# Stick-breaking attention on one Trainium2 core: the causal mask added by VectorE in PSUM instead of by bf16 mask products on TensorE

## The reference, cut to what matters

```
z = einsum('bhtd,bhsd->bhts', qb, kb) * scale
strict = s_idx < t_idx
log_1m = where(strict, log_sigmoid(-z), 0.0)
suffix = cumsum(log_1m, axis=3, reverse=True) - log_1m
a = where(strict, exp(log_sigmoid(z) + suffix), 0.0)
out = einsum('bhts,bhsd->bhtd', a, vb)
```

## Time and profile before

| | before |
|---|---|
| median of 3 runs | 1301.5 us |
| the profiled execution's own time | 1301.93 us |
| its span | 1299.9 us |
| TensorE busy | 1281.9 us, 99% |
| VectorE busy | 883.7 us, 68% |
| ScalarE busy | 688.1 us, 53% |
| GpSimd busy | 110.7 us, 9% |

### The profile page before, as it was taken

One profiled execution on the slowest core, in us unless ns is written; L12 is line 12 of the kernel. 1 busy time (PEld: TensorE's weight loads), 2 busy tenths in 40 slices (PEclk: granted clock), 3 DMA queues, 4 the chain that ended last, 5 costly groups with the idle time before them and its releaser, 6 DMA issues.

```text
span 1299.9 us, 17608 instructions
## 1 busy us (share of the span) xinstructions
PE 1281.9 (99%) x7273; PEld 1106.5 (85%) x7273; DVE 883.7 (68%) x1038; ACT 688.1 (53%) x961; POOL 110.7 (9%) x176
## 2 busy tenths in 40 slices
PE   7999999999999999999999999999999999999999
PEld 7888897988888888888888888898877888888887
DVE  4656664776666776875676666768785566887775
ACT  5755544544444656564554444565566654654453
POOL 6200100100000100030100000101330003000000
PEclk9999999999999999999999999999999999999999
DMA  8754643565555553353365555563544435365552
GB/s 265 258 162 157 204 146 126 178 194 195 193 186 185 181 163 129 131 192 132 130 195 193 189 186 183 182 193 106 162 147 147 160 130 194 131 204 186 193 195 97
DMA packets 156112, 223.62 MB, mean 172 GB/s; under 512 B 6103, under 2 KB 107635, under 8 KB 156032
## 3 DMA queue, kind: packets, MB, share of 16 engines
q1 hardware_dynamic: 154240, 218.18, 51.0%
q0 software_dynamic: 1664, 4.27, 1.0%
q10 hardware_dynamic: 128, 0.05, 0.0%
HBM read 221.44 MB, written 1.05 MB: 171 GB/s over the span
## 4 chain that ended last, share of the span: by engine, by line
PE 85%; DVE 7%; ACT 4%; issue 2%; POOL 1%; DMA 1%; SPq 0%; POOLq 0%; ACTq 0%; DVEq 0%
PE ps L422 18%; PE ps L424 9%; PE ps L472 8%; PE ps L474 7%; PE ps L473 7%; PE ps L407 5%; PE ps L409 5%; PE ps L408 5%; PE ps L606 4%; PE ps L607 4%; PE ps L608 4%; DVE wlo L1691 3%; ACT whi L1149 2%; PE ps L493 1%; PE ps L541 1%
## 5 line engine op out<-in xcount | busy, mean ns | idle before, releaser
L1691 DVE TENSOR_TENSOR wlo<-raw,whi 128x1024 fp32r<-128x1024 f32 x409 | 491.6, 1231 | 167.9 <-ACT whi L1149 165.1
L1149 ACT ACTIVATE whi<-raw 128x1024 fp32r<-128x1024 f32 x412 | 425.5, 1052 | 334.7 <-PE ps L422 156.1
L422 PE MATMUL ps<-RR,whi 128*128 128x512 f32 x1024 | 353.8, 396 | 0.7 <-DVE ar L1794 0.7
L424 PE MATMUL ps<-RR,wlo 128*128 128x256 f32 x1024 | 264.8, 279 | 0.1
L472 PE MATMUL ps<-whi,RR 128*128 128x512 f32 x592 | 238.2, 402 | 2.1 <-DVE RR L1968 0.4
L474 PE MATMUL ps<-whi,RR 128*128 128x512 f32 x592 | 231.0, 390 | 0.0
L473 PE MATMUL ps<-wlo,RR 128*128 128x512 f32 x592 | 230.9, 390 | 0.0
L422 PEld LDWEIGHTS ps<-RR,whi 128*128 128x128 f32 x1024 | 184.8, 188 | 36.3 <-DVE ar L1794 1.0
L424 PEld LDWEIGHTS ps<-RR,wlo 128*128 128x128 f32 x1024 | 193.0, 188 | 11.9 <-DVE RR L1721 0.4
L407 PE MATMUL ps<-RR,whi 128*128 128x256 f32 x512 | 147.4, 288 | 1.5 <-DVE RR L1721 1.4
L409 PE MATMUL ps<-RR,wlo 128*128 128x256 f32 x512 | 144.8, 283 | 0.0
(11 more groups left out here) (338 smaller groups left out, 1266.7 us busy)
## 6 DMA issues: line engine op xcount, KB each, us to landing
raw<-in_ffn_w_gate_up SPq DMA_DIRECT2D x44, 1024.0 KB, 5.1
raw<-in_ffn_w_down SPq DMA_DIRECT2D x33, 1024.0 KB, 5.0
raw<-in_w_in SPq DMA_DIRECT2D x28, 1024.0 KB, 5.1
raw<-in_ffn_w_up SPq DMA_DIRECT2D x22, 1024.0 KB, 5.1
raw<-in_xa_w_kv SPq DMA_DIRECT2D x16, 1024.0 KB, 5.2
raw<-in_sb_w_qkv SPq DMA_DIRECT2D x12, 1024.0 KB, 5.1
raw<-in_ml_w_in SPq DMA_DIRECT2D x11, 1024.0 KB, 6.5
raw<-in_xa_w_q SPq DMA_DIRECT2D x8, 1024.0 KB, 5.3
```

The source lines that it names most:

```text
L422: m = pe.matmul(two(ps[:, bank, :]), p.hi[:, k, :], XT2[:, k, :, :], start=k == 0, stop=k == 7)
L424: pe.matmul(ps[:, bank, 0:256], p.lo[:, k, :], X.h[:, k, :], start=False, stop=False)
L1149: act.activation(p.hi, p.raw, ACT.Copy).then_inc(S["w_hi"], 1)
L1691: dve.tensor_tensor(p.lo, p.raw, p.hi.bitcast(F32), ALU.subtract).then_inc(S["w_lo"], 2 if p.n == 2 else 1)
```

## The change

- On TensorE the four mask products of each pair go. The first score product now starts the bank (`start=True`).
- On VectorE a new function `sb_mask(p)` adds `mStr` to both diagonal squares of both banks in one instruction, 128 partitions by 512 columns, read from PSUM and written back to PSUM, with the bf16 mask broadcast over the four squares. It waits until all scores of the pair are there (`sb_z`), and counts a new semaphore `sb_m`.
- On ScalarE `sb_logs(p)` waits for `sb_m` instead of `sb_z`.
- GpSimd builds `mStr` the other way round, since it is no longer transposed by a product. Same instructions.
- In VectorE's program, `sb_mask(p)` stands in front of `sb_sums(p)`, or of `sb_turned(p-1)` with `sb_sums(p)` right behind it. Around pair 4, one low part of a piece is made ahead of the mask and one behind it.

```diff
             def sb_scores(p):
...
                 for o, r in both:
-                    pe.matmul(o[:, 0:128], mStr[:, :], identb[:, :], start=True, stop=False, skip_group_check=True)
-                    pe.matmul(o[:, 256:384], mStr[:, :], identb[:, :], start=False, stop=False, skip_group_check=True)
-                for o, r in both:
-                    m = pe.matmul(o[:, 128:384], qT[r, p, 128:256], kT[r, p, :], start=False, stop=False, skip_group_check=True)
+                    m = pe.matmul(o[:, 128:384], qT[r, p, 128:256], kT[r, p, :], start=True, stop=False, skip_group_check=True)
                 m.then_inc(S["sb_z"], 1)
...
             def sb_logs(p):
-                act.wait_ge(S["sb_z"], 3 * p + 3)
+                act.wait_ge(S["sb_m"], p + 1)
...
+            def sb_mask(p):
+
+                b = 4 + 2 * (p % 2)
+                diagonal = ps[:, b:b + 2, :].rearrange("p b (x c) -> p b x c", c=128)[:, :, 0:3:2, :]
+                dve.wait_ge(S["sb_z"], 3 * p + 3)
+                dve.tensor_tensor(diagonal, diagonal, mStr[:, :].unsqueeze(1).unsqueeze(1).to_broadcast([128, 2, 2, 128]),
+                                  ALU.add).then_inc(S["sb_m"], 1)
...
             dve.wait_ge(*at("ones", 2))
+            dve.wait_ge(*at("masks", 3))
+            sb_mask(0)
             sb_sums(0)
             sb_k(1)
+            sb_mask(1)
             sb_sums(1)
...
             past("sbv0b")
+            sb_mask(2)
             sb_turned(1)
             sb_sums(2)
...
             lo_to(end("sbk2") - 1 + NSP)
+            sb_mask(3)
             sb_turned(2)
             sb_sums(3)
             sb_k(2)
+            lo_to(end("sbq3") - 1 + NSP)
+            sb_mask(4)
             past("sbq3")
             sb_turned(3)
...
             sb_rest(2)
+            sb_mask(7)
             sb_turned(6)
             sb_sums(7)
...
-            for m, cm, st_, base in ((mInc, -1, 1, 0), (mStr, -1, 1, -1), (mRow, 1, -1, 0)):
+            for m, cm, st_, base in ((mInc, -1, 1, 0), (mStr, 1, -1, -1), (mRow, 1, -1, 0)):
```

More of the change, by code:

```diff
@@ L29 @@
 ml_z mlv_act mlv_dve mo_add mt n_T n_hi n_lo n_r n_sq n_x out pa_m pa_r pa_sq pool_step resid row_in0 row_in1
-row_in2 row_in3 row_in4 row_in5 sb_a sb_c sb_hi sb_k sb_ln sb_lo sb_q sb_t sb_v sb_w sb_z sbv_act sbv_dve
+row_in2 row_in3 row_in4 row_in5 sb_a sb_c sb_hi sb_k sb_ln sb_lo sb_m sb_q sb_t sb_v sb_w sb_z sbv_act sbv_dve
 tm_first w_first w_hi w_lo w_raw0 w_raw1 w_raw2 w_used x_in0 x_in1 xe xm xo xo_hi xp xq xs xt xv xw ya_hi
@@ L1993, in vector_program @@
             sb_rest(1)
+            sb_mask(5)
             sb_turned(4)
@@ L1998, in vector_program @@
             past("sbv1b")
+            sb_mask(6)
             sb_turned(5)
```

## The result

The changed kernel takes 1307.95 us in the median of six runs (1306.70 to 1308.68), the kernel before 1301.56 us (1301.32 to 1301.82). The ratio is 1.0048, with a 95% interval of 1.0035 to 1.0061: slower, by 6.4 us. A second set of five runs, beside the last experiments, gives 1308.6 against 1301.73 us, 1.0049 (1.0037 to 1.0062).

What follows compares the result with a forecast made beforehand. TensorE was taken to bound the attention stage until the masks lengthen the VectorE-ScalarE loop, making sb_turn(7) 5.2 us later, TensorE's 1.9 us saving lost in waits. 1301.5 + 5.2 = 1306.7 us; 8-in-10 range 1303.2 to 1309.6 us.

Steps and rivals of the forecast that it cites:

- TensorE sets the pace, with little room for the loop of the other two: Attention stage before the change: TensorE waits for no engine; VectorE has 21.6 us idle, with 0.8 us slack at sb_turn(7).
- 0.24 us per pair, 1.9 us in all, from the products: Time TensorE saves when its mask products go: 0.24 us per pair, 1.9 us for eight pairs.
- 0.70 us per mask: Length of each added VectorE mask addition, 128x512 in PSUM, taken from the nearest profile row at 0.68 us.
- The upper bound of 1.23: Longest length allowed for one mask, from the 128x1024 form: 1.23 us, giving 1310.9 us in all.
- The walk, 5.2 us: Instruction lengths added from mask 0 to sb_turn(7): 89.35 us, so sb_turn(7) starts at 550.3 us, 5.2 us later.
- The place, not the work: The masks' place in VectorE's queue makes ScalarE's logarithms late; the added 5.6 us of VectorE load alone would fit.
- The clock almost nothing: TensorE stops for up to 2.7 us; a lower granted clock got almost no chance, 0.05 together with slow PSUM.
- one 2.7 us wait near the start of the span: TensorE's longest earlier stop, 2.7 us, said to have left the granted clock where it was.
- The rival that the work only moves to the engine with room: VectorE hides the masks in its 21.6 us idle, TensorE saves 1.9 us: 1299.6 us; chance 0.10.
- Partly hidden: Some masks are reached earlier or are shorter: 1 to 3.5 us later than before, 1302.5 to 1305 us; chance 0.10.
- slow writes to PSUM: A mask nearer 1.2 us than 0.7: 1309.6 to 1311 us; chance 0.05 together with the clock.
- products that were free: Score products start no earlier without TensorE's masks, so it saves nothing; time the same 1306.7 us; no chance given.

Runs made afterwards that it cites:

- e8: The changed kernel with every mask added twice on VectorE, one instruction behind the other: 1314.4 us, ratio 1.0095 to the kernel before.
- e7: The changed kernel with the four mask products per pair back on TensorE beside VectorE's masks: 1307.89 us, ratio 1.0047 to the kernel before.
- e1: The changed kernel with the causal mask left out on both engines: 1299.7 us, ratio 0.9984 to the kernel before.
- e10: The changed kernel with idle TensorE products inside both long waits, eight at sb_scores(4), nine at sb_turn(7): 1306.81 us, ratio 1.0039 to the kernel before.
- e2: The changed kernel with masks in the same places but covering 2 columns of each square instead of 128: 1302.56 us, ratio 1.0005 to the kernel before.
- e3: The changed kernel with six of the eight full-size masks moved forward in VectorE's queue: 1300.21 us, ratio 0.9989 to the kernel before.
- e9: e3 with one low part made ahead of the mask of pair 5, in VectorE's idle time: 1299.58 us, ratio 0.9985 to the kernel before.
- e11: e3 with three idle ScalarE copies ahead of the exponential of pair 7, so that TensorE stops: 1304.33 us, ratio 1.0015 to the kernel before.
- e12: The changed kernel once more, unchanged, beside the other runs on their chip: 1308.6 us.
- e5: The changed kernel with nine idle TensorE products right before sb_turn(7): 1307.19 us, ratio 1.0041 to the kernel before.
- e6: The changed kernel with only the mask of pair 7 moved forward into VectorE's idle time: 1305.15 us, ratio 1.0028 to the kernel before.
- e4: e3 with one low part put ahead of VectorE's copy of the values tile behind pair 5: 1300.07 us, ratio 0.9988 to the kernel before.

## Why the prediction was right, and where it was short

- *TensorE sets the pace, with little room for the loop of the other two*: right. No wait before, five after, and any work on VectorE in the loop shows in full (e8) while work on TensorE hardly shows (e7).
- *0.24 us per pair, 1.9 us in all, from the products*: right. e1 measures 2.0.
- *0.70 us per mask*: right, 0.692 in the mean of eight, over a range of 0.687 to 0.699. The row that it was taken from has 0.683. That this row differs from the mask in the output's place alone, as the prediction says, is not so: the second operand (bf16, broadcast) and the type of the output (fp32r) differ too. An addition of the same size in the kernel before that writes SBUF (L1768, 128x512) takes 0.691 us, so nothing here shows a cost of the output in PSUM. The upper bound of 1.23 was far off.
- *The walk, 5.2 us*: right at every step within 0.1 us; only its start, mask 0, came 0.2 us earlier than forecast. `sb_turn(7)` came at 550.20, forecast 550.3; the waits were 0.7, 2.1, 0.2, 1.4 and 2.6 us, forecast 0.8, 2.1, 0.3, 1.3 and 2.7. e10, which takes the clock away and leaves the rest, measures 5.1.
- *The place, not the work*: shown by e2 (places without work, 2.9 us over e1) and e3 and e9 (work without the places, no loss). The 7 us between e9 and the changed kernel without its clock losses (1306.7 to 1306.8) are all order: e9 has the same eight masks at the same length.
- *The clock almost nothing*: this is the term that was mis-sized. I took one 2.7 us wait near the start of the span as a sign that such stops are harmless, because the profile has the clock in full in every slice. That was a misreading. The wait ends at 8.1 us, and the clock records of that trace start only at 11.9 us; ahead of them the profile shows full clock for want of a record. The products behind the wait took as long as the same kind of product does at the lower level. These are the 16 behind the wait, those of `sb_turn` in the kernel before, and those of `sb_turn(7)` in e8, where the granted share is 0.50 (ns min/median/max, first and last start):

```profile
L493 PE MATMUL ps<-ident,xn x16: 421/421/474, 8.1 to 11.3; 128*128 128x128 f32 x16
L775 PE MATMUL ps<-ident,ar x48: 270/272/273, 472.4 to 545.7; 128*128 128x128 f32 x48
L772 PE MATMUL ps<-ident,ar x5: 417/417/445, 556.6 to 557.5; 128*128 128x128 f32 x5
```

So TensorE ran at the lower level behind that wait, and the row says nothing for harmless stops; whether the clock was already low ahead of it, nothing shows. The other runs show that a fall is a matter of chance: six of 11 runs of e11, five of the first six of the changed kernel and four of five in e12 have a lower mean clock. A fall behind `sb_turn(7)` cost 1.6 us, and falls are what brings the median from 1306.7 to 1307.95.
- *The rival that the work only moves to the engine with room*: false as the change stands, and true in e9. The rule of the Trainium skill ("Perfetto Trace Analysis", Identifying the Most-Contended Engine) is to improve the engine with the highest occupancy first; TensorE is to be judged there not by its products but by its share of peak throughput and by its weight loads, and with 85% it leads by the latter too. The rule gave the right sign only once the receiving engine's queue was ordered for it: ratio 0.9985 in e9 against 1.0048. It has no term for that order.
- *Partly hidden, slow writes to PSUM, products that were free*: none of the three was seen. e1 rules out the last one, 0.692 us the second.

What stays open is why a given stop brings the clock down in one run and not in the next. No run here varies anything that could tell.

## What to carry to other kernels

Before moving work to an engine with idle time, look at which instructions its idle time stands ahead of, and add up the loop that the moved piece joins, in the queue's order; a new first link in a chain over two engines has to be placed where its input gets ready, not where its output is used. When the sum of such a loop comes out longer than the pace of the bounding engine, the difference is the loss; here it could be worked out from one trace to within 0.2 us of the runs without clock losses. Count with the clock too: here a dense TensorE stream with a stop of about two microseconds lost up to another 1.6 us around it, and most of the clock loss was absorbed where TensorE had to wait again later. And before a row is taken as a sign about the clock, check that clock records exist at its time, and compare the length of its products with the same products elsewhere.

## What the hardware showed that was not expected

- TensorE's clock can fall from 2.4 to 1.2 GHz with stops as short as 1.75 us (e7). In the profiled runs the fall begins between 0.2 us before and 1.4 us after TensorE went on from such a stop, and lasts 3.4 us. Behind `sb_turn(7)` it costs 1.6 us, a little less than half of that time. Behind `sb_scores(4)` the profiled runs with such a fall lie 0.3 to 1.0 us above the runs of the same kernel, or of e10, without one (e5, e6, e7), because a later wait takes most of it up. In the kernels whose stops in this stage were 1.6 us or shorter in the profile (e1, e2, e3, e4, e9, e10) it was not seen, and all of their 60 runs have a mean clock of 1.0.
- It is not the same in every run of one program: e11 falls into two groups 1.6 us apart.
- A VectorE addition that reads and writes PSUM is as fast as one that reads PSUM and writes SBUF: 0.692 us for 128x512 with a bf16 second operand broadcast over four squares, against 0.683 (L1968) and 0.691 (L1768) in the kernel before.
